# Cross attention with probabilities normalised in place and a turned output, in an fp32 model kernel on one core

## The reference, cut to what matters

```
def mem_cross_attention(h, mem_n, w_q, w_kv, w_o):
    B, S, _ = h.shape
    q = (h @ w_q).reshape(B, S, CA_HEADS, CA_HEAD_DIM)
    k, v = jnp.split(mem_n @ w_kv, 2, axis=-1)
    ...
    logits = jnp.einsum('bshd,bmhd->bhsm', q, k).astype(jnp.float32) * (CA_HEAD_DIM ** -0.5)
    p = jax.nn.softmax(logits, axis=-1)
    o = jnp.einsum('bhsm,bmhd->bshd', p.astype(v.dtype), v).reshape(B, S, D_MODEL)
    return o @ w_o
```

## Time and profile before

| what | value |
|---|---|
| median of 3 runs | 2574.65 us (2573.97 to 2575.54) |
| the profiled execution: its own time | 2575.51 us |
| its span | 2573.7 us |
| PE busy | 2487.2 us (97%) |
| DVE / ACT / POOL busy | 1316.6 / 1085.1 / 76.5 us |
| mean granted clock of TensorE | 0.990 |
| transfers | 546.07 MB, mean 212 GB/s |

### The profile page before, as it was taken

The page is one execution under the profiler, slowest core; times in us unless marked ns, Lnnn a source line. Parts: engine busy times, 40 slices in busy tenths (PEclk is TensorE's granted clock), DMA queues, the critical chain, the costliest instruction groups (busy, mean ns, idle before and its releaser), DMA issues.

```text
span 2573.7 us, 32905 instructions
## 1 busy us (share of the span) xinstructions
PE 2487.2 (97%) x11876; PEld 1856.2 (72%) x11876; DVE 1316.6 (51%) x1910; ACT 1085.1 (42%) x1640; POOL 76.5 (3%) x123
## 2 busy tenths in 40 slices
PE   8999998899998999999999999999999999999998
PEld 6876433586442678888888888888788888788887
DVE  5644111464122566555556746555556555765554
ACT  4453111352110564454455445445444444644443
POOL 0000000100000100000000000000000000000000
PEclk9999999999999999999999999999999999999999
DMA  7548999648999635365442255555545554353653
GB/s 241 193 136 335 375 409 409 258 139 339 386 409 409 237 111 179 123 227 184 158 172 99 82 173 183 182 184 172 169 160 181 191 196 155 115 177 125 223 187 106
DMA packets 149979, 546.07 MB, mean 212 GB/s; under 512 B 17047, under 2 KB 17248, under 8 KB 149736
## 3 DMA queue, kind: packets, MB, share of 16 engines
q1 hardware_dynamic: 144664, 526.04, 57.4%
q0 software_dynamic: 4912, 17.43, 2.2%
q10 hardware_dynamic: 288, 1.05, 0.1%
HBM read 543.39 MB, written 2.63 MB: 212 GB/s over the span
## 4 chain that ended last, share of the span: by engine, by line
PE 58%; DVE 5%; ACT 2%; issue 2%; ACTq 0%; POOLq 0%; DVEq 0%; POOL 0%
PE bank L2295 17%; PE bank L2297 17%; PE bank L2296 17%; PE bank L2376 2%; DVE low_w L1324 2%; PE bank L2987 1%; PE bank L2872 1%; PE bank L2902 1%; ACT high_w L845 1%; PE bank L2730 1%; ACT tmp L1125 1%; DVE y L1399 0%; PE bank L2327 0%; PE bank L2889 0%; DVE h L1489 0%
## 5 line engine op out<-in xcount | busy, mean ns | idle before, releaser
L2295 PE MATMUL bank<-high_w,xh 128*128 128x512 f32 x2112 | 847.6, 401 | 34.0 <-DVE low_w L1324 17.5
L1324 DVE TENSOR_TENSOR low_w<-stage_w,high_w 128x1024 fp32r<-128x1024 f32 x528 | 641.1, 1223 | 418.5 <-ACT high_w L845 391.5
L2297 PE MATMUL bank<-high_w,xl 128*128 128x512 f32 x2112 | 829.7, 393 | 0.0
L2296 PE MATMUL bank<-low_w,xh 128*128 128x512 f32 x2112 | 829.0, 393 | 0.0
L845 ACT ACTIVATE high_w<-stage_w 128x1024 fp32r<-128x1024 f32 x528 | 554.5, 1058 | 209.8 <-PE bank L2297 184.9
L2295 PEld LDWEIGHTS bank<-high_w,xh 128*128 128x128 f32 x2112 | 400.5, 190 | 132.0 <-issue 27.3
L2297 PEld LDWEIGHTS bank<-high_w,xl 128*128 128x128 f32 x2112 | 400.2, 189 | 86.1
L2296 PEld LDWEIGHTS bank<-low_w,xh 128*128 128x128 f32 x2112 | 401.3, 190 | 78.6
L1734 DVE TENSOR_TENSOR qk<-qk,bank 128x256 f32<-128x256 f32 x32 | 13.5, 421 | 225.3 <-ACT qk L1010 225.3
L2295 PE MATMUL bank<-high_d,hidden_h 128*128 128x512 f32 x320 | 124.9, 390 | 0.0
L2297 PE MATMUL bank<-high_d,hidden_l 128*128 128x512 f32 x320 | 124.5, 389 | 0.0
(11 more groups left out here) (335 smaller groups left out, 2794.1 us busy)
## 6 DMA issues: line engine op xcount, KB each, us to landing
stage_w<-in_wide SPq DMA_DIRECT2D x592, 512.0 KB, 4.4
pair_w<-in_wide SPq DMA_DIRECT2D x128, 512.0 KB, 13.6
stage_d<-in_down SPq DMA_DIRECT2D x120, 512.0 KB, 4.3
proj<-in_wide SPq DMA_DIRECT2D x64, 512.0 KB, 12.9
pair_d<-in_down SPq DMA_DIRECT2D x64, 512.0 KB, 14.6
proj<-in_down SPq DMA_DIRECT2D x32, 512.0 KB, 14.3
gain<-in_gains POOLq DMA_DIRECT2D x18, 512.0 KB, 5.3
skew<-bias_dram POOLq DMA_DIRECT2D x1, 1536.0 KB, 16.8
```

The costliest lines, as they stand in the source:

```text
L1324: vec.tensor_tensor(low_w[:, w], stage_w[:, w], high_w[:, w].bitcast(F32), ALU.subtract)\
L2295: pe.matmul(o, hi, wh, start=start, stop=False)
L2296: pe.matmul(o, hi, wl, start=False, stop=False)
L2297: return pe.matmul(o, lo, wh, start=False, stop=stop)
```

## The change

1. **Cross attentions, DVE.** `scale_probs(j)` takes the reciprocal of the sums and multiplies the exponentials in `tmp`, in place in SBUF, right behind the maximum of head j. PE's `turn_probs` now waits for it (`probs_final`). `take` is not used.
2. **Cross attentions, PE.** `head` uses the values as the stationary operand, so that the output comes with the features on the partitions. `turn_half` is not used, nor is `y`. ACT and DVE split the output of each head from its bank (`keep_head`).
3. **Order.** The first output block moves into `attention`, between the last heads' steps. Without fill in the last step, `keep_clock` is gone as well.
4. **Exits of the mixtures.** `first_turns` is gone; `turn_stage` issues the same transposes, now behind the end of the branch. In `last_down` the loop over the two weight pieces is outside the one over the two output halves.

```
+                def scale_probs(j):
+                    dve.wait_ge(exped, s.soft + j + 1)
+                    link(vec.reciprocal(stat[:, 80 + 2 * j:82 + 2 * j], stat[:, 48 + 2 * j:50 + 2 * j]))
+                    for t in range(T):
+                        e = tmp[:, j % 2 * 1024 + t * S:][:, 0:S]
+                        ins = vec.tensor_scalar(e, e, stat[:, 80 + 2 * j + t:81 + 2 * j + t], None, ALU.mult)
+                    ins.then_inc(probs_final, 1)
+
+                def keep_head(j):
+                    dve.wait_ge(kept_h, kept(s.turn) + j + 1)
+                    vec.tensor_tensor(head_part(xl, j), bank[2 + j % 2][:, :], head_part(xh, j).bitcast(F32),
+                                      ALU.subtract).then_inc(kept_l, 1)
...
@@ DVE, the steps
+                    elif turned_out(s):
+                        scale_probs(j)
+                        if j >= 2:
+                            keep_head(j - 2)
                     elif j >= 2:
                         take(j - 2)
                     after_pieces(each[j])
                 after_pieces(each[H])
-                if C == 1:
+                if turned_out(s):
+                    keep_head(H - 2)
+                    keep_head(H - 1)
+                elif C == 1:
...
@@ ACT, the steps
+                def keep_head(j):
+                    act.wait_ge(turned, 4 * s.turn + j + 1)
+                    act.activation(head_part(xh, j), bank[2 + j % 2][:, :], ACT.Copy).then_inc(kept_h, 1)
...
                     after_pieces(each[j])
+                    if turned_out(s) and j >= 2:
+                        keep_head(j - 2)
                 after_pieces(each[H])
+                if turned_out(s):
+                    keep_head(H - 2)
+                    keep_probs(H - 1)
+                    keep_head(H - 1)
+                    return
...
@@ PE, head
+                    if turned_out(s):
+                        if j >= 2:
+                            pe.wait_ge(kept_l, kept(s.turn) + j - 1)
+                        for d in range(2):
+                            for kt in range(T):
+                                at = 2048 + j * dv + d * P
+                                mm = pe.matmul(bank[2 + j % 2][:, d * S:(d + 1) * S], v[:, kt, at:at + P],
+                                               slot[:, kt * S:(kt + 1) * S], start=kt == 0, stop=kt == T - 1)
+                        mm.then_inc(turned, 1)
+                        return
...
@@ PE, behind the last step
+                if turned_out(s):
+                    out = after(after(s))
+                    def rows(t, p):
+                        pe.wait_ge(kept_h, kept(s.turn) + p + 1)
+                        pe.wait_ge(kept_l, kept(s.turn) + p + 1)
+                        if p == 0:
+                            pe.wait_ge(taken[t], out.out)
+                        piece(bank[4 + t], out.wide, t, p, 0)
+                    head(H - 2)
+                    rows(0, 0)
+                    rows(0, 1)
+                    turn_probs(H - 1)
+                    rows(1, 0)
+                    head(H - 1)
+                    rows(1, 1)
+                    for p in range(2, WP):
+                        for t in range(T):
+                            rows(t, p)
+                    return
...
@@ PE, last_down
-                    for side in range(2):
-                        for p in range(DP):
-                            pe.wait_ge(landed_md[u][p], 32 * PAIRS * (s.moe + 1))
+                    for p in range(DP):
+                        pe.wait_ge(landed_md[u][p], 32 * PAIRS * (s.moe + 1))
+                        for side in range(2):
...
@@ PE, end of sparse and of every
-                first_turns(s)
...
@@ PE, turn_stage
                 if not s.early:
-                    if not first:
-                        turn(s.turn, src, 0, ready(0), left)
+                    turn(s.turn, src, 0, ready(0), left)
...
-                    if not first:
+                    if first:
+                        turn(s.turn, src, 1, ready(1))
+                    else:
                         pending[0, WP - 1] = lambda: turn(s.turn, src, 1, ready(1))
```

More of the change, by code:

```diff
@@ L86, in keys_in, with turned_out, heads_taken @@
     return s.which == "diff"
+def turned_out(s):
+    return s.which == "cross"
+def heads_taken(s):
+    return sum(a.n_heads for a in PLAN[:PLAN.index(s)] if a.kind == "attention" and not turned_out(a))
 def v_piece_of(i):
@@ L438, in y_part, with head_part, finals_before @@
             return v[:, 4 * half:4 * half + 4, t * P:(t + 1) * P]
+        def head_part(v, j):
+            return v[:, 2 * j * S:2 * (j + 1) * S]
+        def finals_before(s):
+            return sum(a.n_heads for a in PLAN[:PLAN.index(s)] if a.kind == "attention" and (a.comps == 2 or turned_out(a)))
         def by_chunk(b):
@@ L1251, in _ @@
                     if s.by_half:
-                        keep_half(s, 1)
+                        if not turned_out(PLAN[PLAN.index(s) - 1]):
+                            keep_half(s, 1)
                     elif s.src == "norm" and late(norm_of(s)) and not norm_of(s).fused:
@@ L2318, in turn_half @@
                 else:
-                    pe.wait_ge(head_taken, a.heads + a.n_heads // 2 * (half + 1))
+                    pe.wait_ge(head_taken, heads_taken(a) + a.n_heads // 2 * (half + 1))
                 pe.wait_ge(kept_h, kept(s.turn))
@@ L2420, in turn_stage @@
                     turn(s.turn, src, 1, ready(1), left)
-            def first_turns(s):
-                n = rows_after(s)
-                for t in range(T):
-                    turn(after(n).turn, yv, t, (folded, t + 2) if n.folded else (normed, 2 * n.norm + t + 1))
             def turn_early(s):
@@ L2460, in residual @@
                             wait_kept(PLAN[PLAN.index(s) - 1].turn + 1)
+                        if half == 0 and turned_out(PLAN[PLAN.index(s) - 2]):
+                            continue
                         if half == 0 and PLAN[PLAN.index(s) - 1].by_half:
```

27 lines of the change are left out of this document (16 added, 11 removed).

## The result

The changed kernel takes 2560.53 us (median of 4 runs, 2557.07 to 2561.61), the kernel before on the same chip 2574.68 us (2573.97 to 2575.54). The ratio is 0.9942, 95% interval 0.9929 to 0.9955: 14.1 us less, where 13.2 were forecast. The profiled execution has a span of 2559.8 us and an own time of 2561.61.

What follows compares the result with a forecast made beforehand. PE, busy for 97% of the span, was taken as the bound. Savings of 5.7 + 4.4 + 0.3 + 3.4 = 13.8 us gave 2560.8, shaded to a forecast of 2561.5 us; 8-in-10 range 2557.5 to 2569.5.

Steps and rivals of the forecast that it cites:

- The hole as a fetch: Mixture exits: PE's idle 2.75 and 2.50 us behind the transposes is an instruction fetch at the jump's target.
- Rival 4: Exits: the change does nothing there, since PE waits for DVE's low pieces; 3.7 us remain, 2571.0 us; chance 0.06.
- 5.7 us for the two holes: Exits: with the jump before the transposes, `scatter` covers the fetch, saving 2.97 and 2.72 us; ends 3.6 and 5.7.
- Rival 2: Exits: the fetch only moves in front of the transposes, saving 3.6 us there, no clock gain; 2567.3 us; chance 0.16.
- 4.4 us for the clock: Behind the exits: without the holes PE's clock stays full, saving 2.8 and 1.6 us; ends 0 and 4.4.
- rival 1: Exits: holes close but the clock still falls, from idle time around the first transposes; 2565.2 us; chance 0.18.
- 0.3 us for `last_down`: Exits: both halves of the first weight piece run during the second's transfer, saving 0.15 us per exit; ends 0 and 1.9.
- 3.4 us for the cross attentions: Four attention ends: each loses 2.6 us of PE work and adds waits of 0.65 and 1.1 us, saving 0.85.
- The far end, 10.4 without waits: Cross attentions: upper end of their saving, 10.4 us over all four if the added waits fall away.
- The scaling's cover: Cross attentions, steps 0 to 2: scaling costs nothing, as DVE's idle 2.57 us exceeds the 1.85 us needed.
- rival 5: Cross attentions: scaling delays DVE's low pieces, PE waits 1.85 us per step once idle falls below that; 2590 us; chance 0.03.

Runs made afterwards that it cites:

- the last batch: The changed kernel unaltered, its near-jump version and its version with head splitting moved in ACT's and DVE's queues, beside the kernel before (2572.65 us); unaltered 2564.79 us.
- the attention's part alone: Kernel before with only the cross attention part of the change, both mixture exits as they were: 2572.4 us, ratio 0.9979.
- the near jump: Kernel before with PE's loops for the never-taken dense branch left out, so the jump's target is close; transposes still ahead of it: 2566.35 us, ratio 0.9958.
- the transposes alone: Kernel before with only the exits' transposes moved behind the jump, `last_down` as it was: 2565.53 us, ratio 0.9958.
- the near jump in the changed kernel: Changed kernel with PE's code for the never-taken branch left out: 2561.52 us, ratio 0.9953 to the kernel before.
- the moved splitting: Changed kernel with the splitting of heads 0 and 1 moved forward in ACT's and DVE's queues: 2556.3 us, ratio 0.9922; repeated, 2554.18 us, 0.9932.

## Why the prediction held

**The forecast** of 2561.5 us is 1.0 us above the measured median. Over all ten executions of the changed kernel the median is 2561.2, lowest 2554.5 and highest 2567.5; in the last batch alone it was 2564.8. So the total fits, with some luck in it (below).

**The hole as a fetch.** Right, and shown four ways: it goes when the target is near; it goes when the transposes are behind the jump; the packet moves under `scatter` with the jump; and it stays with the attention's part alone. Rival 4, the low pieces, falls by the near jump. The Trainium skill (Runtime: NRT & Kernel Launch, Instruction fetch mechanics) says that a taken branch beyond the pages held on chip stalls on a transfer; the runs agree, with a hole of 2.5 and 2.75 us for the far target and none for the near one.

**5.7 us for the two holes.** Right: by the rows of the transposes alone and of the kernel before they were 3.0 and 2.8, forecast 2.97 and 2.72. Rival 2 (3.6) is out, since the sequencer did reach the jump while `scatter` ran. What the prediction had wrong is what is late next. It looked at the low halves for p2 and p3, which were in time, and not at ACT: its square, for which it waits on DVE, and three copies stand ahead of L923, and 1.15 us go back there. The cover was also thinner than "can't start before 851.67 anyway" had it, by 0.4 and 0.7 us, which the near jump in the changed kernel shows to be free.

**4.4 us for the clock.** Mis-sized in this pair of traces, since the clock fell at the first exit for 3.4 us. By the prediction's own prices the first exit gained 2.8 - 1.6 = 1.2 and the second 1.6, 2.8 in all. What the prediction called rival 1 is half true in single executions. In the eight traces with the transposes behind a far jump there are 16 exits, and the clock falls at five of them, for 3.4 us each; in the two traces with the hole (the kernel before, the cross attentions alone) it falls at all four, for 3.4 to 6.8 us. With a near jump, before or after the change, it falls at one of four. What decides at an exit without a hole stays open.

**0.3 us for `last_down`.** By the rows 2 x 0.17 = 0.3 up to the first piece, in the medians nothing.

**3.4 us for the cross attentions.** Measured 3.1 in the trace, and the same with them alone. The prediction counted waits from start to start, and so must the comparison: forecast 0.65 and 1.1, measured 0.82 and 1.07. The work removed was forecast at 2.6 and is 2.64 to 2.68, as the moved splitting shows. So both terms were near, and the sum is 2.65 - 1.9 = 0.8 per attention. The far end, 10.4 without waits, is what the moved splitting reached, 10.6 by its trace.

**The scaling's cover.** "Costs nothing" was right, but its point of decision, in rival 5, was wrong. It said that PE waits once DVE's idle time before the first low piece is below 1.85 us. With that time at zero in step 0, and the low piece 1.4 us later, PE did not wait. I put that down to low pieces that DVE has finished ahead of PE; how many there are was not tried. The order of the output block was the real condition: without it the same scaling costs 1.53 us of wait per attention and the gain of the cross attentions is lost.

**Luck in the total.** The stretches that the change touches gave 10.9 us in the first pair of traces, where the prediction summed 13.8: 1.15 of the 2.9 are the new wait for ACT, 1.6 the fall of the clock at the first exit. The parts add up: 5.8 for the holes, 2.8 for the clock, 0.3 for the loops and 3.1 for the cross attentions, less 1.15, are 10.9. The other 3.0 us came from stretches that the change does not touch. Without them the changed kernel would have come out at about 2563.5, 2 us above the forecast. Such differences fell in the changed kernel's favour in the first pair and, by the medians (7.9 us), against it in the last batch; by that batch's ratio (10.5) they were about nothing.

## What to carry to other kernels

Where a hole of PE stands behind a branch, look at the instruction queue before believing the releaser that the view names, and put the branch where PE, once it has passed its last wait ahead of the branch, still has more work queued than the hole is long. Here 2.84 us of queued work did not quite cover the fetch; what was left of it was free only because DVE set the time from there. Where a stage's work is cut from PE, follow the in-order queues of ACT and DVE to the instruction that PE waits for next: two lines of order there were worth 7.5 us by the traces, more than twice what the new products had brought. In a kernel that is bound by PE, read each part of a change from its own stretch of the trace, since the clock moves the total by as much as the change.

## What the runs showed of the hardware

**The total follows the clock.** The ten executions of the changed kernel, with their mean granted clock: 2554.5 at 0.995, 2557.07 at 0.994, 2558.39 at 0.993, 2560.17 to 2561.61 at 0.992, 2564.54 and 2565.09 at 0.991, 2565.03 at 0.990 and 2567.5 at 0.989. That is (2567.5 - 2554.5) / 6 = 2.2 us for 0.001. The same program on the same data lost the clock at other places of the run each time: in its first trace at 480.0 and 609.7 but not near 1418 or 1817, in the second at the latter two and not at the former.

**A fetch at a far target** took 2.5 to 3.0 us (3.04 in the row of the cross attentions alone) of PE's time when nothing hid it. With `scatter` ahead of it 0.3 to 0.8 us still showed, over the 16 exits with the transposes behind a far jump. The packet began 0.95 to 1.2 us behind the start of the group that PE's last wait let go, at all exits with a far jump but those of the cross attentions alone (1.56) and of the transposes alone, where `scatter` shows no wait. In the changed kernel it began at 846.38, while the last six of `scatter`'s matmul records (845.40 to 848.24) ran; the jump stands behind them, so the sequencer had passed all six by then. The Trainium skill (TensorE: Matmul & The Clock Gate, the table at its head) gives PE a queue of 64 instructions. The trace agrees as far as these six go, and no run here shows where the queue ends.

**A wait costs more than its idle time in the view.** The two waits of 0.59 and 0.79 us, 1.38 together, cost 0.82 and 1.07, 1.9 us. The view counts from the modelled end of the last matmul. A row of the block is 0.39 us long while the next one starts 0.23 behind it, so 0.16 are missed at a wait. And the first matmul of the block behind a wait takes 0.47 us by its row instead of 0.39, another 0.08.
